# Inverting the delta rule's triangles on 32x32 diagonal blocks instead of whole 128x128 tiles

## The reference

```
kk = jnp.einsum("bhncd,bhnmd->bhncm", k, k)
a_mat = jnp.where(strict, kk * beta[..., :, None] * decay, 0.0) + jnp.eye(c, dtype=jnp.float32)
rhs = jnp.concatenate([v * beta[..., None], k * (beta * jnp.exp(gc))[..., None]], axis=-1)
sol = lax.linalg.triangular_solve(a_mat, rhs, left_side=True, lower=True, unit_diagonal=True)
u, w = sol[..., :dv], sol[..., dv:]
```

## Time and profile before

| | us |
|---|---|
| median of 3 runs | 3393.42 |
| lowest and highest | 3391.13, 3393.49 |
| profiled execution, its own time | 3396.17 |
| its span, first to last instruction | 3394.4 |
| mean granted clock of TensorE | 0.99 |

### The profile page before, as it was taken

One profiled execution on the slowest core, in us unless ns is written; L12 is line 12 of the kernel. 1 busy time (PEld: TensorE's weight loads), 2 busy tenths in 40 slices (PEclk: granted clock), 3 DMA queues, 4 the chain that ended last, 5 costly groups with the idle time before them and its releaser, 6 DMA issues.

```text
span 3394.4 us, 42945 instructions
## 1 busy us (share of the span) xinstructions
PE 3296.8 (97%) x18368; PEld 2691.9 (79%) x18368; DVE 1607.4 (47%) x2534; ACT 1137.8 (34%) x1838; POOL 333.7 (10%) x568
## 2 busy tenths in 40 slices
PE   7999999999999999999999999999999899999999
PEld 5887978888788878887886577888888786677886
DVE  5747544434542553444227644434434426554444
ACT  6547332222443431222235533211112336432222
POOL 1101000000210010000000103100001301030000
PEclk9999999999999999999999999999999899999999
DMA  4102032242125424222325331221022213012321
GB/s 136 50 26 75 1 100 75 75 146 90 53 99 181 168 87 142 82 75 69 84 74 210 100 100 50 75 75 66 11 74 69 57 44 94 25 50 100 123 75 37
DMA packets 190733, 282.00 MB, mean 83 GB/s; under 512 B 19144, under 2 KB 122056, under 8 KB 190416
## 3 DMA queue, kind: packets, MB, share of 16 engines
q1 hardware_dynamic: 188368, 272.19, 24.2%
q10 hardware_dynamic: 2176, 7.08, 0.6%
HBM read 274.01 MB, written 2.10 MB: 81 GB/s over the span
## 4 chain that ended last, share of the span: by engine, by line
PE 89%; ACT 4%; DVE 4%; POOL 2%; issue 1%; DMA 1%; ACTq 0%; DVEq 0%; POOLq 0%; SPq 0%
PE ps L820 11%; PE ps L821 10%; PE ps L822 10%; PE ps L538 6%; PE ps L539 6%; PE ps L540 6%; PE ps L851 5%; PE ps L852 5%; PE ps L853 5%; PE ps L434 4%; PE ps L613 2%; PE ps L614 2%; PE ps L615 2%; PE ps L1446 2%; PE ps L1414 1%; PE ps L2169 1%
## 5 line engine op out<-in xcount | busy, mean ns | idle before, releaser
L443 ACT ACTIVATE R<-ring 128x2048 fp32r<-128x2048 f32 (+4 forms) x285 | 401.5, 1420 | 1001.9 <-PE ps L822 351.2
L820 PE MATMUL ps<-R,R 128*128 128x512 f32 (+1 forms) x1760 | 652.6, 371 | 8.5 <-DVE R L1309 3.8
L821 PE MATMUL ps<-R,R 128*128 128x512 f32 (+1 forms) x1760 | 650.0, 369 | 0.0
L822 PE MATMUL ps<-R,R 128*128 128x512 f32 (+1 forms) x1760 | 649.9, 369 | 0.0
L538 PE MATMUL ps<-R,R 128*128 128x512 f32 (+1 forms) x1016 | 398.7, 392 | 19.4 <-DVE ringlo L634 10.6
L820 PEld LDWEIGHTS ps<-R,R 128*128 128x128 f32 x1760 | 332.9, 189 | 70.1 <-DVE R L1309 4.6
L539 PE MATMUL ps<-R,R 128*128 128x512 f32 (+1 forms) x1016 | 382.5, 376 | 0.0
L540 PE MATMUL ps<-R,ringlo 128*128 128x512 f32 (+1 forms) x1016 | 381.7, 376 | 0.0
L822 PEld LDWEIGHTS ps<-R,R 128*128 128x128 f32 x1760 | 333.1, 189 | 55.9
L821 PEld LDWEIGHTS ps<-R,R 128*128 128x128 f32 x1760 | 333.1, 189 | 54.4
L756 DVE TENSOR_TENSOR R<-ring,R 128x2048 fp32r<-128x2048 f32 x88 | 203.5, 2317 | 304.9 <-ACT R L443 304.9
(11 more groups left out here) (295 smaller groups left out, 4645.9 us busy)
## 6 DMA issues: line engine op xcount, KB each, us to landing
ring<-in_w_mod SPq DMA_DIRECT2D x24, 2048.0 KB, 9.8
ring<-in_ffn_w_in SPq DMA_DIRECT2D x44, 1024.0 KB, 12.1
ring<-in_w_ffn_in SPq DMA_DIRECT2D x44, 1024.0 KB, 12.3
ring<-in_ffn_w_out SPq DMA_DIRECT2D x10, 2048.0 KB, 7.8
ring<-in_w_ffn_out SPq DMA_DIRECT2D x10, 2048.0 KB, 7.9
ring<-in_dil_w_in SPq DMA_DIRECT2D x9, 2048.0 KB, 7.9
ring<-in_gdn_w_in SPq DMA_DIRECT2D x8, 2048.0 KB, 8.9
ring<-in_w_in SPq DMA_DIRECT2D x6, 1536.0 KB, 9.6
```

Of the source, the lines that this page charges most:

```text
L443: return act.e.activation(o, i, fn, **kw)
L820: pe.e.matmul(ps, w[0], x[0], start=(k == 0), stop=False)
L821: pe.e.matmul(ps, w[0], x[1], start=False, stop=False)
L822: t = pe.e.matmul(ps, w[1], x[0], start=False, stop=(k == 7))
```

## The change

The 16 triangles of a half are seen as two groups (g) of eight blocks (b, two heads by four chunks). Of each 128x128 triangle the four diagonal blocks of 32x32 are packed: quadrant r of the partitions (32 of them, `QU[r]`) holds diagonal block r, and eight triangles lie side by side in 256 columns. TP holds both the inverse (index 0) and its transpose (index 1), so that nothing is turned any more between levels. AB is the buffer of the triangles, TB the transposed inverse TT (in the place of k_), seen by group and block.

- `pe_small` makes the diagonal blocks and their transposes by matmuls with the identity; `dve_small` masks them and subtracts them from the identity, which is level 0.
- Levels 1 to 4: `pe_masked`, 32 matmuls of 32x32 a group; `dve_masked`, 128x256; `pe_grown`, 64 matmuls (inverse and transpose); `dve_grown`, 128x512. Each small matmul uses the sixteenth of the array that its partitions fix: rows r of the array for the operands, columns r for the result, so that four neighbours in the program lie on its diagonal.
- Pairs (32 to 64): `pe_pairs_masked` and `pe_pairs_grown` with off-diagonal blocks, evacuated by VectorE and ScalarE, one each.
- Halves (64 to 128): `pe_halves_masked` and `pe_halves_grown`, 64x64 matmuls.
- GpSimd, which had nothing in this stage, sets the buffers to zero and copies the finished diagonal blocks into T64 and TB.
- The turns of keys and values no longer stand ahead of the inverse but between its steps, and so do the key tails on VectorE and the value weighing on ScalarE. The splits of z move on ScalarE between the value weighings and on VectorE behind the inverse. The 12 constant matmuls are gone, and the constants that are loaded are smaller.

The diff, cut to that (left out: what moves in the boot, names of arguments, and the old functions, which stand in the kernel above):

```diff
-N_GDN = 7 * 128 + 128 + 512
+N_GDN = 7 * 32 + 128 + 512
...
+    low, up = i % 32, np.arange(32)[None, :]
+    for n, r, c in ((0, low, up), (0, up, low), (1, low, up), (2, low, up), (3, low, up), (4, low, up)):
         b = 1 << n
-        k[:, g:g + 128] = (i // (2 * b) == j // (2 * b)) & (i % (2 * b) >= b) & (j % (2 * b) < b)
-        g += 128
+        k[:, g:g + 32] = (r // (2 * b) == c // (2 * b)) & (r % (2 * b) >= b) & (c % (2 * b) < b)
+        g += 32
...
-        T, TT, W, Z, oraw, EGR = v, k_, DT, AT, v, ktl
+        TT, W, Z, oraw, EGR = k_, DT, AT, v, ktl
+        QU = [slice(32 * i, 32 * i + 32) for i in range(4)]
+        TP = arena(bufs[7], 4, 8, 32).rearrange("p (g w) b c -> p g w b c", w=2)
+        XP, X5 = arena(bufs[7] + 1024, 2, 8, 32), arena(bufs[7] + 1536, 2, 8, 32)
+        T64, X64 = arena(bufs[6], 2, 8, 64), arena(bufs[6] + 1024, 2, 8, 64)
+        AB, TB = arena(bufs[8], 2, 8, 128), arena(bufs[1], 2, 8, 128)
...
-            steps_ = [(n, h) for n in range(7) for h in range(4)]
-            pe_masked(hg, *steps_[0])
-            for i, (n, h) in enumerate(steps_):
-                if i + 1 < len(steps_):
-                    pe_masked(hg, *steps_[i + 1])
-                pe_level(hg, n, h)
-                if i and 1 <= steps_[i - 1][0] < 6:
-                    pe_turn(hg, *steps_[i - 1])
+            pe_small(hg, 0)
+            pe_small(hg, 1)
+            pe_keys_turned(hg, 0)
+            pe_keys_turned(hg, 1)
+            pe_masked(hg, 1, 0)
+            pe_keys_turned(hg, 2)
+            pe_masked(hg, 1, 1)
+            pe_keys_turned(hg, 3)
+            pe_grown(hg, 1, 0)
+            pe_grown(hg, 1, 1)
+            for n in range(2, 5):
+                pe_masked(hg, n, 0)
+                pe_masked(hg, n, 1)
+                if n < 4:
+                    pe_values_turned(hg, n - 2)
+                pe_grown(hg, n, 0)
+                pe_grown(hg, n, 1)
+            pe_pairs_masked(hg)
+            pe_values_turned(hg, 2)
+            pe_pairs_grown(hg)
+            pe_values_turned(hg, 3)
+            pe_halves_masked(hg, 0)
+            pe_halves_masked(hg, 1)
+            pe_halves_grown(hg, 0)
+            pe_halves_grown(hg, 1)
...
+        def pe_keys_turned(hg, c):
+            ps = bank("k turned", hg, c)
+            pe.wait_ge(*at("k beta", hg, 3))
+            tp([(hs4(ps, h), sl4(k_, h, c)) for h in range(4)]).then_inc(*pe.done("k turned", hg, c))
+
+        def pe_values_turned(hg, c):
+            ps = bank("v turned", hg, c)
+            pe.wait_ge(*at("silu", hg, 11))
+            tp([(hs4(ps, h), sl4(v, h, c)) for h in range(4)]).then_inc(*pe.done("v turned", hg, c))
+
+        def pe_small(hg, g):
+            ps = bank("small", hg, g)
+            pe.wait_ge(*at("ak", hg, 2 * g))
+            pe.wait_ge(*at("ak", hg, 2 * g + 1))
+            for b in range(8):
+                for i, r in enumerate(QU):
+                    pe.e.matmul(ps[r, 32 * b:32 * b + 32], AB[r, g, b, r], ident[r, r], start=True, stop=True)
+                for i, r in enumerate(QU):
+                    t = pe.e.matmul(ps[r, 256 + 32 * b:288 + 32 * b], ident[r, r], AB[r, g, b, r], start=True, stop=True)
+            t.then_inc(*pe.done("small", hg, g))
+
+        def pe_masked(hg, n, g):
+            ps = bank("mask", hg, n, g)
+            pe.wait_ge(*at("t", hg, n - 1, g))
+            for b in range(8):
+                for r in QU:
+                    t = pe.e.matmul(ps[r, 32 * b:32 * b + 32], AB[r, g, b, r], TP[r, g, 0, b, :], start=True, stop=True)
+            t.then_inc(*pe.done("mask", hg, n, g))
+
+        def pe_grown(hg, n, g):
+            ps = bank("level", hg, n, g)
+            pe.wait_ge(*at("masked", hg, n, g))
+            for b in range(8):
+                for r in QU:
+                    pe.e.matmul(ps[r, 32 * b:32 * b + 32], TP[r, g, 1, b, :], XP[r, g, b, :], start=True, stop=True)
+                for r in QU:
+                    t = pe.e.matmul(ps[r, 256 + 32 * b:288 + 32 * b], XP[r, g, b, :], TP[r, g, 1, b, :],
+                                    start=True, stop=True)
+            t.then_inc(*pe.done("level", hg, n, g))
+
+        def pe_pairs_masked(hg):
+            ps = [bank("pair mask", hg, e) for e in range(2)]
+            pe.wait_ge(*at("t", hg, 4, 0))
+            pe.wait_ge(*at("t", hg, 4, 1))
+            for g, b in itertools.product(range(2), range(8)):
+                n = 256 * g + 32 * b
+                for e in range(2):
+                    t = pe.e.matmul(ps[e][QU[2 * e + 1], n:n + 32], AB[QU[2 * e], g, b, QU[2 * e + 1]],
+                                    TP[QU[2 * e], g, 0, b, :], start=True, stop=True)
+                    if (g, b) == (1, 7):
+                        t.then_inc(*pe.done("pair mask", hg, e))
+
+        def pe_pairs_grown(hg):
+            pt = bank("pair t", hg)
+            ps = [bank("pair tt", hg, e) for e in range(2)]
+            pe.wait_ge(*at("pair masked", hg, 0))
+            pe.wait_ge(*at("pair masked", hg, 1))
+            for g, b in itertools.product(range(2), range(8)):
+                n, last = 256 * g + 32 * b, (g, b) == (1, 7)
+                t = pe.e.matmul(pt[QU[1], n:n + 32], TP[QU[1], g, 1, b, :], X5[QU[1], g, b, :], start=True, stop=True)
+                if last:
+                    t.then_inc(*pe.done("pair t", hg))
+                for e in range(2):
+                    o = QU[2 * e + 1]
+                    t = pe.e.matmul(ps[e][QU[2 * e], n:n + 32], X5[o, g, b, :], TP[o, g, 1, b, :], start=True, stop=True)
+                    if last:
+                        t.then_inc(*pe.done("pair tt", hg, e))
+
+        def pe_halves_masked(hg, g):
+            ps = bank("half mask", hg, g)
+            pe.wait_ge(*at("t half", hg))
+            pe.wait_ge(*at("t block", hg, 1))
+            for b in range(8):
+                t = pe.e.matmul(ps[64:128, 64 * b:64 * b + 64], AB[0:64, g, b, 64:128], T64[0:64, g, b, :],
+                                start=True, stop=True)
+            t.then_inc(*pe.done("half mask", hg, g))
+
+        def pe_halves_grown(hg, g):
+            ps = bank("half tt", hg, g)
+            pe.wait_ge(*at("tt pair", hg, 1))
+            pe.wait_ge(*at("tt block", hg, 3))
+            pe.wait_ge(*at("half masked", hg, g))
+            for b in range(8):
+                t = pe.e.matmul(ps[0:64, 64 * b:64 * b + 64], X64[64:128, g, b, :], TB[64:128, g, b, 64:128],
+                                start=True, stop=True)
+            t.then_inc(*pe.done("half tt", hg, g))
+
...
+            z = z_pieces(hg)
+            act_split(z[0], WHZ[hg])
+            act_values_weighed(hg, 0)
+            act_split(z[1], WHZ[hg])
+            act_values_weighed(hg, 1)
+            act_split(z[2], WHZ[hg])
+            o = QU[3]
+            act.wait_ge(*at("pair mask", hg, 1))
+            activate(X5[o, :, :, :], by_block(PS.of("pair mask", hg, 1))[o], ACT.Copy, scale=-1.0).then_inc(
+                *act.done("ps", "pair mask", hg, 1))
+            act.mark("pair masked", hg, 1)
+            o = QU[2]
+            act.wait_ge(*at("tt zero", hg))
+            act.wait_ge(*at("pair tt", hg, 1))
+            activate(TB[o, :, :, 96:128], by_block(PS.of("pair tt", hg, 1))[o], ACT.Copy).then_inc(
+                *act.done("ps", "pair tt", hg, 1))
+            act.mark("tt pair", hg, 1)
...
+            dve_small(hg, 0)
+            dve_small(hg, 1)
+            dve_masked(hg, 1, 0)
+            dve_keys_tailed(hg, 0)
+            dve_masked(hg, 1, 1)
+            dve_keys_tailed(hg, 1)
+            dve_keys_tailed(hg, 2)
+            dve_grown(hg, 1, 0)
+            dve_grown(hg, 1, 1)
+            for n in range(2, 5):
+                dve_masked(hg, n, 0)
+                dve_masked(hg, n, 1)
+                if n == 2:
+                    dve_keys_tailed(hg, 3)
+                dve_grown(hg, n, 0)
+                dve_grown(hg, n, 1)
+            o = QU[1]
+            dve.wait_ge(*at("pair mask", hg, 0))
+            dve.e.tensor_scalar(X5[o, :, :, :], by_block(PS.of("pair mask", hg, 0))[o], -1.0, 0.0, M, A_).then_inc(
+                *dve.done("ps", "pair mask", hg, 0))
+            dve.mark("pair masked", hg, 0)
...
+        def dve_keys_tailed(hg, c):
+            tail = TL[:, c, hg * 4:hg * 4 + 4].unsqueeze(2).broadcast_to([128, 4, 128])
+            dve.wait_ge(*at("q decayed", hg, 3))
+            dve.wait_ge(*at("tail", hg))
+            dve.wait_ge(*at("k beta decayed", hg, c))
+            dve.e.tensor_tensor(c4(ktl, c), p4(PS.of("k turned", hg, c)), tail, M).then_inc(
+                *dve.done("ps", "k turned", hg, c))
+            dve.mark("k tailed", hg, c)
+
+        def dve_small(hg, g):
+            both = GM[:, 0:2, :].unsqueeze(2).broadcast_to([128, 2, 8, 32])
+            one = GM[:, 6:7, :].unsqueeze(2).broadcast_to([128, 2, 8, 32])
+            dve.wait_ge(*at("gm"))
+            dve.wait_ge(*at("kk", hg, 3))
+            dve.wait_ge(*at("small", hg, g))
```

(82 more changed lines are left out.)

98 lines of the change are left out of this document (32 added, 66 removed).

## The result

| | before | after |
|---|---|---|
| median, us | 3393.45 (16 runs) | 3401.41 (16 runs) |
| lowest and highest | 3389.68, 3401.12 | 3395.60, 3405.28 |
| profiled execution, its own time | 3396.17 | 3398.52 |
| its span | 3394.4 | 3396.7 |

The ratio of after to before is 1.002 (95% interval 1.0012 to 1.0028): 8.0 us slower by the medians. The forecast was 3333 us with a range of 3320 to 3402 and 0.75 on faster. So the kernel is slower where faster was forecast. The number lies at the upper edge of the range, where the text had put a rival with a different mechanism.

The account below looks back on a forecast made before the run. TensorE's pace was taken to bound the inverse stage: 65.0 us falling to 35.0 in each half, 60.0 us less than the profiled 3396.17, so 3336.2; with the runs' median 2.75 lower, 3333 us, range 3320 to 3402.

Parts of the forecast that it names:

- What bounds the kernel, what goes: Inverse stage, 65.0 us per half of the heads: bounded by TensorE's pace; of 552 records only 32 transposes stay.
- The price p of a small record: Time per 32x32 matmul record on TensorE: 7 to 14 ns, 10.5 in the middle, with four diagonal tiles running together.
- The instruction queue brings 16 KB packets ... and I have no row that shows one late.: Instruction supply: 144 packets in the whole span, 12 more a stage after the change; priced at nothing.
- The stage at p = 7: New inverse stage at 7 ns a record, summed from entry to halves: 31.3 us, next product at 157.1.
- Entry: Start of the stage, diagonal blocks of both groups: 7.3 us, with TensorE idle 2.9 us for VectorE's line 1977.
- Level by level: Levels one to four of the inverse at p = 7: 4.7, 4.1, 4.1 and 3.3 us, with VectorE shared by two groups.
- the middle forecast: Stage with p midway between 7 and 14 ns: 35.0 us, for both halves 60.0 us less.
- The clock: Rival: TensorE's clock at its lower level throughout a stage, 47.5 us a stage, kernel 3358 us; chance 0.05.
- The other side: Rival: diagonal tiles not running together (one PSUM bank), or issue slower than 25.9 ns; 3401 to 3515 us; chance 0.21.
- Priced at nothing: GpSimd's copies (at most 7.0 us) and zeroing, z splits and value weighing hidden under other work; smaller constant load saves nothing.

Follow-up runs that it names:

- e3_long: The changed kernel with 20 long matmuls a stage put in (128x128 weights, 512 columns, results unread): 3393.0 us, ratio 0.9996.

## Why the prediction was wrong

- **What bounds the kernel, what goes.** Right: the stage was TensorE's, and its 552 records went.
- **The price p of a small record.** 7 to 14 ns, 10.5 in the middle; measured 8.9 at the full clock and 13.4 at the lower. This term, on which the whole sum hung, was right, and so was the 27.9 ns for one tile (29 measured). The tiles run together although all four write one bank of PSUM. The Trainium skill, "TensorEngine Tiling (Array Packing)", Restrictions and Gotchas, rules that out for different row tiles. The Trainium skill, "TensorE: Matmul & The Clock Gate", Part 1, sets about 25 ns between starts. Taken for tiles that differ in rows and columns, either would forbid this pace, and the measurement decides against both; for records on one tile the 29 ns agree with the second.
- **The step that failed: "The instruction queue brings 16 KB packets ... and I have no row that shows one late."** I counted bytes over the span, found 12 packets a stage more of 0.3% of the DMA engines, and took that as nothing. I should have asked how fast the packets are used up. Before, 128 records at 0.1115 us were 14.3 us a packet; at p = 7 to 14 ns they are 0.9 to 1.8. A block comes in 3.7 us, which is 29 ns a record however cheap the record is. Up to the pairs a stage has 1,816 records with its turns, 14 blocks or 52 us, and that stretch lasted 53.5. Pairs and halves, bounded by the array at the lower clock, take the other 13.
- **The stage at p = 7.** Entry: the wait for VectorE was 2.6 us (2.9 forecast) and no more. Level by level the sum was made of VectorE's chain, 3.3 to 4.7 us; a level was 11.2 us, three blocks. Up to the pairs the middle forecast had 27 us and the trace shows 53.5. Of these, 19.0 are pauses with "issue"; and with the clock up and the pauses partly filled (e3_long) this part took no less, so the clock is not what made it long.
- **The clock.** A rival with 0.05, as the result of idle time. It fell in both stages (0.58 and 0.60), and cost about 4 us a stage, from the pairs on; where it fell without any idle time (one tile) idleness is not the reason, or not alone.
- **The other side.** 3401 was forecast for tiles that wait for a shared bank at 27.9 ns a record. The time came out so because 3.7 us over 128 is 29 ns: nearly the same price from another cause. The number was met by accident and its mechanism refuted.
- **Priced at nothing.** GpSimd's copies, the z splits and the smaller constants are not waited for: the list of TensorE's waits names none of them.

## What to carry to other kernels

Before splitting matmuls into many small ones, count instructions per microsecond beside array time: here a TensorE stream got 128 MATMUL records with their loads per 3.7 us, and cutting instructions (one product and a VectorE transpose for two products) was worth 31 ns a record, two to three times their run time. Pauses named "issue" inside a run of matmuls, at equal counts of records, are the sign. Work with few instructions and much array time fitted into them here for nothing, and held the clock up. A bound that happens to give the measured number is no proof of its mechanism: the counts between the pauses and one burst of constants told supply and shared bank apart.

## What the hardware showed beside it

- Records on four 32x32 tiles of the diagonal, all writing one PSUM bank, go at 8.9 ns each at clock 1.00 and 13.4 ns at 0.50; on one tile at 29 ns and at 42 to 48. In neither case is the pace halved with the clock.
- The clock fell to 0.50 under an unbroken stream of 32x32 matmuls on single tiles (TensorE busy for 15.00 of 15.00 us), and the 20 long matmuls, with which it was 0.95 over the stage in the other order, brought it back there for 10 us only.
- VectorE turns 128x256 float32 in 32x32 blocks in 0.445 us, beside 0.420 for a subtraction of that size from PSUM.
